# Scores of retention and attention as three products of rounded high and low parts, with finer waits at three places

## The reference

```
h = rms_norm(x, mix_norm);  z = h @ w_in            # q, k, v, gates of both mixers
# B: retention, 4 heads, q and k of 256, v of 512
inner = einsum('bcnhd,bcmhd->bchnm', qf, kf) * decay
y_inner = einsum('bchnm,bcmhe->bcnhe', inner, vf)   # and a state over chunks
# A: attention, 8 heads of 128 over 2 key heads, own chunk of 64 and the one before, rotary q and k, sinks
scores = einsum('bcqhgd,bckhd->bchgqk', qc, kb) * Dh ** -0.5
probs = softmax(concat([scores, sink]))[..., :-1];  out = einsum(probs, vb)
x = x + (sigmoid(ga) * y_att + sigmoid(gr) * y_ret) @ w_out
x = x + peer(rms_norm(x))                           # product-key experts, 16384 x 1024 twice
x = x + sigmoid(rms_norm(x) @ w_pg) * (p @ w_pe);  return rms_norm(x)
```

## Time and profile before

| | |
|---|---|
| median of 3 runs | 1984.89 us (1984.79 to 1986.66) |
| the profiled execution | 1985.89 us, of which the span is 1984.1 |
| granted TensorE clock, mean | 0.998 |
| busy share of the span: PE, PEld, DVE, ACT, POOL | 99%, 87%, 69%, 41%, 62% |
| retention | from the first projections to about 417 us |
| rounds of attention | about 474 to 574 us |
| merge and output projection | about 574 to 696 us |
| last transposes of the experts | 1908.7 us |

### The profile page before, as it was taken

The page is one execution under the profiler, slowest core; times in us unless marked ns, Lnnn a source line. Parts: engine busy times, 40 slices in busy tenths (PEclk is TensorE's granted clock), DMA queues, the critical chain, the costliest instruction groups (busy, mean ns, idle before and its releaser), DMA issues.

```text
span 1984.1 us, 27327 instructions
## 1 busy us (share of the span) xinstructions
PE 1958.0 (99%) x10232; PEld 1725.7 (87%) x10232; DVE 1366.9 (69%) x2287; ACT 806.2 (41%) x1272; POOL 1233.6 (62%) x686
## 2 busy tenths in 40 slices
PE   7999999999999999999999999999999999999998
PEld 6888888888888788999999999999888888888887
DVE  6433333342741479998968888861999899999976
ACT  5222222232553333433346666654433333333352
POOL 4343434352234433899996767766998898988842
PEclk9999999999999999999999999999999999999999
DMA  5222222233223232899997999998999999999931
GB/s 198 85 91 85 91 85 85 85 117 112 80 75 96 96 120 83 322 335 352 366 358 268 387 375 362 370 387 277 360 372 360 365 360 353 367 367 363 359 104 43
DMA packets 171953, 471.93 MB, mean 238 GB/s; under 512 B 13776, under 2 KB 62928, under 8 KB 170064
## 3 DMA queue, kind: packets, MB, share of 16 engines
q1 hardware_dynamic: 58032, 209.04, 30.2%
q0 software_dynamic: 41472, 151.01, 20.7%
q10 hardware_dynamic: 72352, 110.64, 15.5%
HBM read 413.49 MB, written 54.53 MB: 236 GB/s over the span
## 4 chain that ended last, share of the span: by engine, by line
PE 94%; DVE 2%; ACT 1%; DMA 1%; issue 0%; ACTq 0%; POOL 0%; POOLq 0%; SPq 0%; DVEq 0%
PE bank L932 29%; PE bank L934 28%; PE bank L933 28%; PE bank L1185 4%; PE bank L1047 1%; PE bank L1130 1%; DMA raw<-weights 1%; PE bank L1115 1%; PE bank L1091 0%; PE bank L1101 0%; DVE bank L1364 0%; DMA xT<-x_cols 0%; ACTq L793 0%; PE bank L1016 0%; PE bank L1138 0%
## 5 line engine op out<-in xcount | busy, mean ns | idle before, releaser
L493 POOL TENSOR_TENSOR w_lo<-raw,w_hi 128x1024 fp32r<-128x1024 f32 x390 | 936.9, 2411 | 655.6 <-ACT w_hi L550 652.1
L932 PE MATMUL bank<-h_hi,w_hi 128*128 128x352 f32 (+2 forms) x1560 | 549.2, 352 | 1.4 <-DVE h_lo L1537 1.4
L934 PE MATMUL bank<-h_hi,w_lo 128*128 128x352 f32 (+2 forms) x1560 | 538.1, 345 | 0.0
L550 ACT ACTIVATE w_hi<-raw 128x1024 fp32r<-128x1024 f32 x390 | 407.6, 1054 | 320.0 <-DMA raw<-weights 271.6
L933 PE MATMUL bank<-h_lo,w_hi 128*128 128x352 f32 (+2 forms) x1560 | 537.2, 344 | 0.0
L932 PEld LDWEIGHTS bank<-h_hi,w_hi 128*128 128x128 f32 x1560 | 293.8, 188 | 21.2 <-DVE h_lo L1537 1.8
L933 PEld LDWEIGHTS bank<-h_lo,w_hi 128*128 128x128 f32 x1560 | 294.7, 189 | 19.7
L934 PEld LDWEIGHTS bank<-h_hi,w_lo 128*128 128x128 f32 x1560 | 293.1, 188 | 20.7
L1753 DVE TENSOR_TENSOR b_lo<-scr,b_hi 128x384 fp32r<-128x384 f32 x128 | 267.7, 2092 | 47.5 <-ACT b_hi L846 47.4
L932 PE MATMUL bank<-w_hi,b_hi 128*128 128x512 f32 x768 | 298.9, 389 | 0.1
L934 PE MATMUL bank<-w_hi,b_lo 128*128 128x512 f32 x768 | 298.8, 389 | 0.0
(11 more groups left out here) (227 smaller groups left out, 2707.5 us busy)
## 6 DMA issues: line engine op xcount, KB each, us to landing
raw<-weights SPq DMA_DIRECT2D x390, 512.0 KB, 6.1
act_scratch<-scr ACTq DMA_DIRECT2D x64, 384.0 KB, 7.0
gate_scratch<-scr ACTq DMA_DIRECT2D x12, 2048.0 KB, 13.1
scr<-gate_scratch ACTq DMA_DIRECT2D x22, 768.0 KB, 11.8
scr<-act_scratch ACTq DMA_DIRECT2D x22, 768.0 KB, 17.4
xT<-gate_scratch ACTq DMA_DIRECT2D x10, 768.0 KB, 9.8
xT<-act_scratch ACTq DMA_DIRECT2D x10, 768.0 KB, 14.5
scr<-scr ACTq DMA_DIRECT2D x20, 128.0 KB, 3.8
```

The lines of the kernel that those rows point to most:

```text
L493: return nc.gpsimd.tensor_tensor(w_lo[:, s, :], raw[:, s, :], w_hi[:, s, :].bitcast(F32), ALU.subtract)
L550: nc.scalar.activation(w_hi[:, u_mod, :], raw[:, u_mod, :], ACT.Copy).then_inc(hi_done, 1)
L932: nc.tensor.matmul(out, a_hi, c_hi, start=first, stop=False)
L934: return nc.tensor.matmul(out, a_lo, c_hi, start=False, stop=last)
```

## The change

Buffers `qk_parts` hold high and low parts of q and k. VectorE makes them: in retention by a copy and a subtraction over 1024 elements for q and for k (`split_pair`), in attention by a second sum that writes the high part and a subtraction (`rotate`). TensorE takes three rounded products instead of one plain one for three of the four column blocks of retention and for three of the four token tiles of attention. The three waits: `p_ready` is signalled and awaited for each token tile, the weights are read ahead only up to 4 + 4 units in the merge, and the last transposes begin with the tiles that are there.

```
@@ buffers
+        with nc.sbuf_tensor("qk_parts", [P, 4, UW], F32R) as qk_parts:
+            pass
+        r_q_hi, r_q_lo, r_k_hi, r_k_lo = (qk_parts[:, n, :].rearrange("p (c t) -> p c t", c=2) for n in range(4))
+        a_q_hi, a_q_lo, a_k_hi, a_k_lo = (qk_parts[:, n, :].rearrange("p (c t) -> p c t", c=2) for n in range(4))
@@ ScalarE, merge
-                run_ahead(UNIT[("ga", KT - 1)] + 4 + m)
+                run_ahead(UNIT[("ga", KT - 1)] + 4 + min(m, 4))
@@ TensorE, scores of retention
-                        ins = nc.tensor.matmul(bank[:, 2 + j, 0:S - P * j], r_k[:, c, P * j:P * j + P],
-                                               r_q[:, c, P * j:S], start=c == 0, stop=c == 1)
+                        out, a, q = bank[:, 2 + j, 0:S - P * j], slice(P * j, P * j + P), slice(P * j, S)
+                        if j < TT - 1:
+                            ins = mm3(out, r_k_hi[:, c, a], r_k_lo[:, c, a], r_q_hi[:, c, q], r_q_lo[:, c, q],
+                                      c == 0, c == 1)
+                        else:
+                            ins = nc.tensor.matmul(out, r_k[:, c, a], r_q[:, c, q], start=c == 0, stop=c == 1)
@@ TensorE, scores and transposes of attention
-                            ins = nc.tensor.matmul(o, q, a_k[:, kv, P * (t - 1):P * (t + 1)], start=True, stop=True)
+                            at, keys = slice(P * t, P * t + P), slice(P * (t - 1), P * (t + 1))
+                            ins = mm3(o, a_q_hi[:, h % 2, at], a_q_lo[:, h % 2, at], a_k_hi[:, kv, keys],
+                                      a_k_lo[:, kv, keys], True, True)
-                    pe.wait_ge(p_ready, h + 1)
                     if h > 0:
                         pe.wait_ge(pT_ready, h)
                     for t in range(TT):
+                        pe.wait_ge(p_ready, TT * h + t + 1)
@@ TensorE, last transposes of the experts
+            pe.wait_ge(y_act_ready, TT - 1)
+            pe.wait_ge(y_dve_ready, TT - 1)
+            for k in range(4):
+                for t in (TDT, 0, 1):
+                    turn_y(k, t)
             pe.wait_ge(y_act_ready, TT)
+            for k in range(4):
+                turn_y(k, TDT - 1).then_inc(yT_done, 1)
             pe.wait_ge(y_dve_ready, TT)
-            for k in range(KT):
+            for k in range(4, KT):
...
@@ VectorE
-                ve.sem_inc(rot_ready, 1)
+            def split_pair(z, hi, lo):
+                step(nc.vector.tensor_copy(hi, z))
+                mark(tt(lo, z, hi.bitcast(F32), ALU.subtract), rot_ready)
+            def rotate(r, dst, hi, lo):
                 z = next_tile()
                 ve.wait_ge(swapped[r % 2], 32 * (r // 2 + 1))
                 step(tt(prod, (k_swap if r < AKV else q_swap)[:, r % 2, :], rope_a[:, 1, :], ALU.mult))
                 step(tt(dst, z, rope_a[:, 0, :], ALU.mult))
+                step(tt(hi, dst, prod, ALU.add))
                 step(tt(dst, dst, prod, ALU.add))
                 ve.sem_inc(tile_free, 1)
-                ve.sem_inc(arot_done, 1)
+                mark(tt(lo, dst, hi.bitcast(F32), ALU.subtract), arot_done)
@@ VectorE, head 0: after end_pair(0, ("rk", 1), r_k)
+            split_pair(r_q, r_q_hi, r_q_lo)
+            split_pair(r_k, r_k_hi, r_k_lo)
@@ VectorE, heads 1 to 3
-                    for kind, dst in (("rq", r_q), ("rk", r_k)):
-                        begin_pair(i, (kind, 2 * i), dst)
-                        end_pair(i, (kind, 2 * i + 1), dst)
-                    transposed_lower(i - 1, range(4))
+                    begin_pair(i, ("rq", 2 * i), r_q)
+                    end_pair(i, ("rq", 2 * i + 1), r_q)
+                    split_pair(r_q, r_q_hi, r_q_lo)
+                    begin_pair(i, ("rk", 2 * i), r_k)
+                    end_pair(i, ("rk", 2 * i + 1), r_k)
+                    transposed_lower(i - 1, (0, 1))
+                    split_pair(r_k, r_k_hi, r_k_lo)
+                    transposed_lower(i - 1, (2, 3))
@@ VectorE, scale of attention
-                    together([lambda t=t: ts(a_s[:, h % 2, t, :], a_s[:, h % 2, t, :], rden[:, t:t + 1], None, ALU.mult)
-                              for t in range(TT)])
-                    ve.sem_inc(p_ready, 1)
+                    for t in range(TT):
+                        ts(a_s[:, h % 2, t, :], a_s[:, h % 2, t, :], rden[:, t:t + 1], None, ALU.mult).then_inc(p_ready, 1)
```

More of the change, by code:

```diff
@@ L1251, in _, with turn_y @@
             up_turn(NKEY // STEP - 1)
+            def turn_y(k, t):
+                return nc.tensor.transpose(bank[:, YT_BANKS[k], P * t:P * t + P], y_tok[:, t, P * k:P * k + P], ident)
+            pe.wait_ge(y_act_ready, TT - 1)
[3 more added lines that the diff above has]
+                    turn_y(k, t)
             pe.wait_ge(y_act_ready, TT)
+            for k in range(4):
+                turn_y(k, TDT - 1).then_inc(yT_done, 1)
             pe.wait_ge(y_dve_ready, TT)
-            for k in range(KT):
+            for k in range(4, KT):
                 if k >= 6:
@@ L1258, in _ @@
                 for t in range(TT):
-                    ins = nc.tensor.transpose(bank[:, YT_BANKS[k], P * t:P * t + P], y_tok[:, t, P * k:P * k + P], ident)
+                    ins = turn_y(k, t)
                 ins.then_inc(yT_done, 1)
@@ L1405, in end_pair @@
                           lambda: tt(dst[:, 1, :], dst[:, 1, :], p2, ALU.add)])
-                ve.sem_inc(rot_ready, 1)
-            def rotate(r, dst):
+            def split_pair(z, hi, lo):
+                step(nc.vector.tensor_copy(hi, z))
+                mark(tt(lo, z, hi.bitcast(F32), ALU.subtract), rot_ready)
+            def rotate(r, dst, hi, lo):
                 z = next_tile()
@@ L1490, in _ @@
             ve.wait_ge(rope_a_landed, 16)
-            rotate(0, a_k[:, 0, :])
+            rotate(0, a_k[:, 0, :], a_k_hi[:, 0, :], a_k_lo[:, 0, :])
             transposed_lower(RH - 1, (2, 3))
-            rotate(1, a_k[:, 1, :])
+            rotate(1, a_k[:, 1, :], a_k_hi[:, 1, :], a_k_lo[:, 1, :])
             add_retention(RH - 1)
@@ L1517, in _ @@
                         ve.wait_ge(sc_done, h - 1)
-                    rotate(h + 2, a_q[:, h % 2, :])
+                    rotate(h + 2, a_q[:, h % 2, :], a_q_hi[:, h % 2, :], a_q_lo[:, h % 2, :])
                 elif i <= AH + 2:
```

## The result

The changed kernel takes 2005.55 us (median of 4 runs, 2005.04 to 2006.04) where the kernel before takes 1985.59 on the same chip: ratio 1.0098, 95% interval 1.0086 to 1.011, slower by 1%. The forecast was 2002.6 with a range of 1992 to 2008. The profiled execution took 2005.71, its span is 2003.9 against 1984.1: +19.8, where the sum said +17.7.

What follows compares the result with a forecast made beforehand. TensorE bounds the kernel (94% of the chain), with VectorE lacking room at three places. +8.0 + 1.7 + 1.4 + 11.9 - 3.0 - 1.4 - 0.9 = +17.7 on 1985.89 gives 2003.6, as median 2002.6 us; range 1992 to 2008.

Steps and rivals of the forecast that it cites:

- Head 0: Retention's first head: splits on VectorE, taking turns with GpSimd, delay the bank for TensorE's third value tile, +8.0 us.
- The slow clock: Behind head 0's gap: TensorE's products run at 1.2 GHz and lose half of 3.4 us, +1.7 (0 to 1.7).
- Heads 1 to 3: Later retention heads: the splits fit where VectorE waits anyway, 0; another lost turn would cost 1.0 in each.
- scores' saving: Retention's scores on TensorE: rounded products for plain ones save 0.76 us a head, 3.0 in four.
- The keys: Rotations of the attention keys: one added operation in each delays the release of the tile, twice 0.72, +1.4 us.
- Attention: Attention slots: the fourth scaling comes 0.13 late, stands behind GpSimd, and most slots grow to 11.35 us; +11.9.
- (a): Rival in attention: the scaling passes ahead of GpSimd, costing about +3 there; total +8.8, 1993.7 us; chance 0.16.
- Merge and last transposes: TensorE's wait for h_lo in the merge goes, -1.4; twelve transposes at the end fill an eviction wait, -0.9 us.
- (d): Rival: VectorE's extra work is covered and TensorE's column counts decide; -7.1, 1977.8 us; chance 0.07.
- (b): Rival in head 0: the splits cost only their 4.1 us and no slow clock; +12.1, 1997.0 us; chance 0.08.
- (e): Rival: both costs small, head 0 at 4.1 and attention slots uncollided; +0.7, no change; chance 0.05.
- (c): Rival in attention: gaps of about 2 us also lower the clock, 1.7 lost in five slots; +26.2, 2011.1; chance 0.06.

Runs made afterwards that it cites:

- the splits moved: Changed kernel with head 0's splits of q and k behind VectorE's remainders of the second and third value tiles: 1994.82 us.
- GpSimd held: Changed kernel with GpSimd's subtraction in each attention slot held until VectorE has scaled the four tiles: 1990.25 us.
- one operation fewer: Changed kernel without the plain sum of dst and prod in each attention rotation, output wrong, only to price the operation: 1989.9 us.
- plain: Changed kernel with attention's scores plain again, without the second sum and remainder in each rotation: 1989.24 us.
- the two waits alone: Kernel before with only the merge's read-ahead limit of 4 units and the early last transposes, no rounded scores: 1983.16 us, ratio 0.9983.
- GpSimd held in head 0: Changed kernel with GpSimd's four subtractions in head 0 held until both splits are done: 2002.11 us.
- one wait per head: Retention alone rounded, splits later, attention plain, with TensorE's wait before attention's last transposes per head instead of per tile: 1979.84 us.

## Why the prediction was right

**Head 0** (+8.0): TensorE goes on at 57.96 instead of 50.33, +7.6. The order of turns was right instruction by instruction (copy ended at 51.85 for 51.9 forecast, subtraction at 55.14 for 55.3, remainder of v from 57.16 for 57.5). That half of it is GpSimd is shown by holding it; that the place is the cause, by moving it.

**The slow clock** (+1.7, range 0 to 1.7): 2.6, outside its own range. The forecast took the length of the one low stretch of before, 3.4 us; here 5.2 us lay behind the restart. As the same wait of 7.5 us had 3.0 to 5.4 us behind it in other kernels (a loss of 1.5 to 2.7), this term could not be foreseen to better than a microsecond. A second low stretch, which the forecast did not have, stands at the keys: products 0.43 us apart from 442.0 to 445.4 behind the wait of 2.7, +1.7; with the splits moved, the same wait had none. The 0.9 and the 1.7 are more than the 2.1 us by which the sum was short.

**Heads 1 to 3** (0): the transposes of heads 1, 2 and 3 start 9.28, 8.51 and 7.76 later than before, each time 0.76 less, so nothing but the **scores' saving** (-0.76 a head) moved. That agrees to the hundredth.

**The keys** (+1.4): the wait went from 1.0 to 2.7, +1.7; as in the earlier trace rows one rotation step stood behind GpSimd (436.00, 2.90 us).

**Attention** (+11.9): +11.9, and 0.6 ahead of it for the first low part of q. Size and mechanism are shown from three sides (GpSimd held, one operation fewer, plain). That the number agrees to the tenth is luck, for two errors cancel inside: seven slots measure 77.0 (10.36, 10.42, then 11.17 to 11.48) for 78.1, but only 0.4 was absorbed at the end, not 1.5. And it is not the fourth tile that is late: GpSimd comes 0.05 to 0.53 us behind the start of the first scaling (554.39 and 554.21, 543.21 and 542.68), and TensorE waits with two or four of its eight transposes done,

```profile
543.97 0.60 PE L1111 MATMUL bank<-small,scr 128*128 128x128 f32 x4
545.78 0.70 PE L1111 MATMUL bank<-small,scr 128*128 128x128 f32 x4 [1.21 <-DVE scr L1559]
```

so the second or third scaling is the one that stands. GpSimd's distance from the rotation's start is the 4.68 forecast (4.69), but the scaling starts 4.15 behind it, in one round 4.50, and not 4.04. The forecast's margin was 0.13 us, as small as this error, which happened to go the way that made the meeting surer; by the forecast's own arithmetic the same error the other way is rival (a). The forecast named waits of 2 us; they are 1.0 to 1.4; that TensorE itself comes later would explain this.

**Merge and last transposes** (-1.4, -0.9): -1.65 for the first both in the kernel with the two waits alone and in the changed one (701.31 to 722.55 is 1.64 less than the +22.9 at the end of attention); for the second -0.4 in the one and -1.4 in the other, which leaves its size open.

Of the rivals, (a), a scaling that passes ahead of GpSimd, is refuted by L1559's 3.26 us; (d), VectorE covered, by the 7.5; (b), four instructions at their own length and no slow clock, by the same 7.5 and the 0.50; (e), both costs small, by both. (c), a falling clock in attention, did not come: the clock is 1.00 there in spite of seven waits of up to 1.4 us. Its price is real, though: with GpSimd held in head 0 the same waits stand in attention, and behind one of them (553.27, 1.4 us) the clock did fall,

```profile
555.50:558.50 3.00, 3.00 (x12) 0.50 0.02 5
```

so the argument against (c), that no slow stretch shows behind a wait of 2.0, proved less than it was taken for.

## What to carry to other kernels

These rules come from this one kernel. Before work is put on VectorE, find where GpSimd's operations fall in its timeline and how far the next dependent VectorE operation over SBUF is from them: if the added length is less than that distance it costs little (here 0.7 us net, at most 2.5), if more it costs a whole GpSimd operation in each round. A wait on the engine that is off the critical path (here GpSimd, until VectorE turns to operations that read a bank) took the meeting away here without a new wait of TensorE. A one-time stall of TensorE should be priced with slow products behind it as a range, here 1.5 to 2.7 us behind a stall of 7.5 us and none or 1.7 behind one of 2 to 3, and not as a fixed sum. Work that only the scores need should be issued behind the releases that the next projection needs.

## What the runs showed of the hardware

- Small operations are held as well: the sum of 128x4 ahead of the scaling, in SBUF on all sides, takes 0.16 us, and 2.22 where GpSimd's operation had started 0.45 ahead of it:

```profile
509.87 2.65 POOL L497 TENSOR_TENSOR w_lo<-raw,w_hi 128x1024 fp32r<-128x1024 f32 x1 [8.88 <-ACT w_hi L554]
510.32 2.22 DVE L1556 TENSOR_TENSOR misc<-misc 128x4 f32<-128x4 f32 x1
```

- The slow clock behind a wait is not fixed by the wait's length. Behind waits of 7.5 us at one place the products ran at 1.2 GHz for 5.2, 5.4, 4.2 and 3.0 us in four kernels, behind one of 3.8 us for 5.3. Behind waits of 2.7 us at the keys it was 3.4 us in the changed kernel and nothing with the splits moved. Behind a wait of 2.0 us it was nothing in the kernel before and a low stretch of 3.4 us with one wait per head; behind the waits of 1.0 to 1.4 us in attention it was nothing in the changed kernel, and 3.4 us behind one of six with GpSimd held in head 0. Part of what parts two executions of one kernel is this.
- Operations of VectorE that read a bank, and a reduction over 1024 elements of SBUF, run beside GpSimd at their own speed (0.69, 1.23 and 1.22 us).
